# A two-block fp32 transformer kernel: the mixer's column groups, its levels' slots and VectorE's sums of weights in another order

## The chip, the cores and the metric

One core of a Trainium2 chip runs the whole program. The metric is the device time of one execution in microseconds (us); lower is better. The kernel before took 2854.26 us (median of 3 runs).

## What is computed

The reference runs 256 tokens of width 2048, all in fp32, through two transformer blocks. The change lies in the second block's mixer, which works on `hx`, the normalized and modulated tokens, and projects them with `w_in`:

```python
ux, vx, qx, kx, vvx, gx, dfx, dbx = split_proj(hx @ w_in)          # ten column groups of 512
# gated linear attention: 4 heads, keys of 128, values of 256, chunks of 128 tokens, both directions
b = jnp.cumsum(gc, axis=2)
scores = einsum('bhid,bhjd,bhijd->bhij', qc, kc, exp(b_i - b_j))
o = scores @ vc + (qc * exp(b)) @ s
s = exp(b_last) * s + (kc * exp(b_last - b))^T @ vc
# gla_out: rms norm of o, times silu(g);  spatial_gating: gelu(u) * (w_s @ layer_norm(gelu(v)) + b_s)
```

The four lines of the attention are the reference's in meaning, written shorter.

## The kernel before, in words

**Matmuls.** Every large product is cut into column groups of 512, and a group into chunks of 512 rows of the weight. A chunk multiplies 2 x 2 blocks with seven products in place of eight (`chunk`, line 533): 14 fp32 matmuls of 128x256 on TensorE. Four of the seven products use a raw block of the weight (`ring`), three use sums of blocks (`sums`), which VectorE makes two chunks ahead in `step(m)`, lines 962 to 967: two additions, a drain, an addition, a drain, an addition, each over 128x512. `step(m)` waits until the weights of chunk m+2 have landed and until TensorE is through with chunk m-1, so it can begin when chunk m begins. When a group's four chunks are done, VectorE puts its products together in `gather` (lines 979 to 989, four instructions).

**The mixer.** Its 40 slots (g, c) are chunk c of group g. `MIX_GROUPS` gives the order of the groups, and the table `MIX_BESIDE` names for each slot the smaller work that stands beside the chunk. All engines walk the same table. TensorE runs the chunk and then the slot's items. VectorE runs `level_open` of the slot's level if it has one, then `step`, then the items in their order. ScalarE and GpSimd run their part of each item. No scheduler is involved: the order is written out, and an engine that waits holds up all that stands behind it.

**Levels.** The decayed scores of a chunk of tokens are built in eight levels, ("level", n, l) with n = 0, 1 the half of the tokens. For l below 7 a level passes through four engines:

1. VectorE, `level_open` (line 1382, two subtractions): differences of the summed decays into `e_buf`;
2. ScalarE (1880 and 1882): absolute value, then exponential (with a table load ahead of it if a silu or gelu came between);
3. VectorE (`level_close`, 1361 and 1394): takes the previous level's scores out of PSUM, then makes `ql`, queries times decay, in two instructions. GpSimd (2132) makes `kl`, keys times decay, in two instructions, from the same exponential;
4. TensorE (869): four matmuls of 128x128 of `kl` and `ql`, once both are ready.

`level_open` of the next level needs `e_buf` free, so it waits for GpSimd. Level 7 has no decay.

**Other items the texts name.** `upd` (TensorE 857, VectorE 1447, eight instructions): the new states, from the values and the decayed keys. `qt` (TensorE 831, ScalarE 1906): the queries turned. `qe` (ScalarE 1885, VectorE 1460): queries times the summed decays. `o` (TensorE 881 and 883, ScalarE 1924): the output of the attention and its squares. `o_sum`, `o_norm` (VectorE 1469, GpSimd 2121 and 2123, VectorE 1476): its norm and the gate. `y` (TensorE 891) and `y_take` (VectorE 1483): the result turned. `v_mean`, `v_sum`, `v_norm` (VectorE 1490 to 1494, 1500, 1506, with ScalarE and GpSimd between): layer norm of v. `sgu`, `sgu_take` (TensorE 903, VectorE 1406): spatial mixing.

## Time and profile before

| | |
|---|---|
| runs | 2854.8, 2851.78, 2854.26 us; median 2854.26 |
| profiled execution | 2853.87 us, its span 2852.1 us |
| TensorE matmul (PE) busy | 2799.4 us, 98% of the span |
| TensorE weight load (PEld) | 2449.2 us, 86% |
| VectorE (DVE) | 2151.4 us, 75% |
| ScalarE (ACT), GpSimd (POOL) | 396.4 us, 353.2 us |
| mean granted TensorE clock | 0.993 |

Each line of the profile's groups names source line, engine, operation and tiles. `idle before` or a bracket such as [1.84 <-DVE mem L1394] is the time the engine stood still just before, and what ended it. An fp32 matmul counts as two rows of the trace. `mem` is the large buffer that most tiles are cut from, `act_t` and `small` are others, `PS` is PSUM.

### The profile page before, as it was taken

What the parts mean: (1) busy time and instruction counts of PE and PEld (TensorE: products, weight loads), DVE (VectorE), ACT (ScalarE), POOL (GpSimd) and SP (SyncE); (2) the same over time, 40 slices, a digit from 0 to 9 for tenths busy, and PEclk for the clock granted to TensorE, in tenths of its full rate; (3) what the DMA queues carried; (4) which work ended last, traced back from release to release, by engine and by line L of the source; (5) the groups of instructions that cost most, each with busy time, mean ns of one, the idle gap of its engine ahead of it and who ended that gap; (6) DMA issues with size and microseconds to landing.
All of it is one profiled execution on the core that took longest, in us unless ns stands there. A gap on an engine that the chain in (4) does not pass through costs nothing.

```text
span 2852.1 us, 34930 instructions
## 1 busy us (share of the span) xinstructions
PE 2799.4 (98%) x13260; PEld 2449.2 (86%) x13260; DVE 2151.4 (75%) x3355; ACT 396.4 (14%) x703; POOL 353.2 (12%) x438
## 2 busy tenths in 40 slices
PE   8999999999999999999999999999799999999998
PEld 7888888888888888888887888788688888888887
DVE  5888777988999999989886558787676676555554
ACT  2221112001111111100012113310200000000000
POOL 1012231011121121211110001110001110000000
PEclk9999999999999999999999999999899999999999
DMA  8677666677776667677874455447467766566553
GB/s 264 214 254 229 207 203 203 211 247 223 210 213 213 208 207 213 207 250 250 277 242 130 143 156 140 125 155 223 141 214 214 219 214 200 170 160 195 177 173 122
DMA packets 274984, 571.62 MB, mean 200 GB/s; under 512 B 24522, under 2 KB 25432, under 8 KB 274304
## 3 DMA queue, kind: packets, MB, share of 16 engines
q1 hardware_dynamic: 244112, 460.44, 52.4%
q0 software_dynamic: 30416, 108.87, 12.2%
q8 instruction: 105, 1.72, 0.2%
q14 instruction: 63, 0.52, 0.1%
q10 hardware_dynamic: 288, 0.07, 0.0%
HBM read 565.37 MB, written 3.93 MB: 200 GB/s over the span
## 4 chain that ended last, share of the span: by engine, by line
PE 74%; issue 18%; DVE 3%; DVEq 1%; DMA 1%; POOL 1%; ACT 1%; POOLq 0%; ACTq 0%
PE PS L533 69%; PE PS L595 1%; DVEq L964 1%; PE PS L561 1%; DMA ring<-in_w_in 1%; PE PS L731 0%; PE PS L647 0%; PE PS L622 0%; DVE sums L965 0%; DVE sums L967 0%; DVE mem L1053 0%; DMA ring<-in_w_down 0%; DVE sums L962 0%; DVE ring L963 0%; PE PS L869 0%
## 5 line engine op out<-in xcount | busy, mean ns | idle before, releaser
L533 PE MATMUL PS<-sums,mem 128*128 128x256 f32 x4080 | 1216.4, 380 | 0.0
L533 PE MATMUL PS<-ring,mem 128*128 128x256 f32 x3800 | 1075.8, 380 | 1.4 <-DVE sums L967 1.4
L533 PEld LDWEIGHTS PS<-sums,mem 128*128 128x128 f32 x4080 | 777.0, 190 | 106.1
L533 PE MATMUL PS<-ring,act_t 128*128 128x256 f32 x3112 | 845.6, 380 | 3.9 <-DVE sums L967 3.3
L533 PEld LDWEIGHTS PS<-ring,mem 128*128 128x128 f32 x3800 | 719.5, 191 | 99.7 <-DVE sums L967 2.5
L533 PEld LDWEIGHTS PS<-ring,act_t 128*128 128x128 f32 x3112 | 585.5, 191 | 82.2 <-issue 4.6
L962 DVE TENSOR_TENSOR sums<-ring 128x512 f32<-128x512 f32 x432 | 314.2, 727 | 382.7 <-PE PS L533 353.9
L1053 DVE SCALAR_TENSOR_TENSOR mem<-mem,small 128x512 f32<-128x512 f32 x480 | 353.8, 758 | 34.0 <-DMA mem<-in_w_mod 2.7
L965 DVE TENSOR_TENSOR sums<-sums,ring 128x512 f32<-128x512 f32 x432 | 312.3, 723 | 33.4 <-issue 1.3
L967 DVE TENSOR_TENSOR sums<-sums,ring 128x512 f32<-128x512 f32 x432 | 307.6, 712 | 33.2 <-issue 1.4
L533 PE MATMUL PS<-sums,act_t 128*128 128x256 f32 x1104 | 329.2, 380 | 0.0
L2024 POOL DMA_DIRECT2D mem<-in_w_mod x192 | 139.3, 726 | 1497.9 <-DVE mem L1053 1411.4
L963 DVE TENSOR_TENSOR ring<-ring 128x512 f32<-128x512 f32 x432 | 295.9, 685 | 0.0
L533 PEld LDWEIGHTS PS<-sums,act_t 128*128 128x128 f32 x1104 | 210.4, 191 | 28.8
L1605 ACT COPY first_q<-PS 128x256 f32<-128x256 f32 x98 | 36.4, 372 | 993.3 <-PE PS L533 993.3
L979 DVE TENSOR_TENSOR mem<-PS,first_q 128x512 f32<-128x512 f32 x96 | 65.7, 685 | 44.6 <-PE PS L533 44.5
L1252 DVE SCALAR_TENSOR_TENSOR mem<-PS,small,mem 128x255 f32<-128x255 f32 x176 | 76.6, 477 | 3.3
L1776 ACT ACTIVATE mem<-PS,small 128x256 f32<-128x256 f32 x88 | 44.8, 560 | 208.7 <-PE PS L595 208.7
L985 DVE TENSOR_TENSOR mem<-PS,mem 128x512 f32<-128x512 f32 x96 | 66.4, 692 | 9.3 <-issue 0.8
L989 DVE TENSOR_TENSOR mem<-PS,mem 128x512 f32<-128x512 f32 x96 | 66.4, 691 | 9.2 <-issue 0.4
L1768 ACT ACTIVATE mem<-mem,small 128x512 f32<-128x512 f32 x44 | 29.4, 714 | 157.4 <-DVE mem L989 157.4
L1626 ACT ACTIVATE act_t<-PS,small 128x256 f32<-128x256 f32 x64 | 28.8, 517 | 160.5 <-PE PS L561 160.3
(237 smaller groups left out, 1224.7 us busy)
## 6 DMA issues: line engine op xcount, KB each, us to landing
ring<-in_w_in SPq DMA_DIRECT2D x240, 512.0 KB, 3.7
mem<-in_w_mod POOLq DMA_DIRECT2D x192, 512.0 KB, 5.0
ring<-in_w_up SPq DMA_DIRECT2D x176, 512.0 KB, 3.8
ring<-in_w_ffn_in SPq DMA_DIRECT2D x176, 512.0 KB, 3.6
ring<-in_w_down SPq DMA_DIRECT2D x88, 512.0 KB, 4.5
ring<-in_w_ffn_out SPq DMA_DIRECT2D x88, 512.0 KB, 3.8
ring<-in_w_out SPq DMA_DIRECT2D x64, 512.0 KB, 4.3
ring<-in_w_branch_a SPq DMA_DIRECT2D x16, 512.0 KB, 3.7
```

The source lines that it names most:

```text
L533: mm = pe.matmul(product(g, j), of(j, 2 * (c if part is None else part) + q), weights(j, n, q), start=lead and j in OPENS, stop=tail, skip ...
L962: ve.tensor_tensor(to[:, 0], b11, b12, ADD)
L963: ve.tensor_tensor(b12, b22, b12, ADD)
L965: ve.tensor_tensor(to[:, 1], to[:, 0], b22, ADD)
L967: ve.tensor_tensor(to[:, 2], to[:, 1], b21, ADD).then_inc(s["sums_ready"], 1)
L979: ve.tensor_tensor(both(c11, c12), two(Q2), bc(first_q[:, g % 2].unsqueeze(1), [P, 2, 256]), ADD)\
L985: ve.tensor_tensor(both(c12, c22), bc(product(g, Q5).unsqueeze(1), [P, 2, 256]), both(c12, c21), SUB)\
L989: ve.tensor_tensor(both(c12, c21), two(Q3), both(c12, c21), ADD).then_inc(s["acc_free"], 1)
L1053: op = ve.scalar_tensor_tensor(acc[:, which, :], wm[:, h % 2, k, :], col, acc[:, which, :], MUL, ADD)
L1252: op = ve.scalar_tensor_tensor(o, src, conv[:, k, 2 * side:2 * side + 1], o, MUL, ADD)
L1776: op = act.activation(dst[:, 2 * part + f, :], PS[:, 7, f * T:(f + 1) * T], ACT.Identity, scale=conv[:, k, 1:2], bias=conv[:, k, 3:4])
L2024: pool.dma_start(wm[:, h % 2], w_mod[:, kt:kt + 2, col:col + CN]).then_inc(wm_loaded[h % 2], 16)
```

## The change

Three edits, all in the mixer.

1. **Groups.** The order k, q, vv0, vv1, g0, ... becomes k, vv0, vv1, q, g0, ...: the values' two groups come before the queries'. With them `upd` moves from slot (4, 0) to (3, 1) and `qt` from (2, 0) to (4, 0). The waits are changed to match.
2. **Slots of the second half's levels.** Level (1, 0) with its `qe` moves from (6, 3) to (6, 2), ahead of that slot's `o_sum` and `o_norm`; level (1, 1) moves from (7, 0) to (6, 3). `y_take` moves from (7, 0) to (7, 1). Levels (1, 2) and later keep their slots.
3. **`step` in two parts.** In a slot with a level VectorE now runs `level_open`, the first two additions (`step_first`), `level_close`, and then the last two additions (`step_last`), where the whole `step` stood ahead of `level_close`. In the other slots both parts follow each other as before. `level_close` also waits for `q_kept`.

```diff
-        MIX_GROUPS = [("k", 2560), ("q", 2048), ("vv0", 3072), ("vv1", 3584), ("g0", 4096), ("g1", 4608),
+        MIX_GROUPS = [("k", 2560), ("vv0", 3072), ("vv1", 3584), ("q", 2048), ("g0", 4096), ("g1", 4608),
...
-                      (1, 3): [("gather", 1), ("cum",)], (2, 0): [("qt",)], (2, 1): [("rem", 0), ("rem", 1)],
-                      (2, 2): [("wst",)], (2, 3): [("gather", 2)], (3, 0): [("wsum",)], (3, 3): [("gather", 3)],
-                      (4, 0): [("upd", 0), ("upd", 1)], (4, 1): [("level", 0, 0), ("qe", 0)],
+                      (1, 3): [("gather", 1), ("cum",)], (2, 1): [("rem", 0), ("rem", 1)],
+                      (2, 2): [("wst",)], (2, 3): [("gather", 2)], (3, 0): [("wsum",)], (3, 1): [("upd", 0), ("upd", 1)],
+                      (3, 3): [("gather", 3)], (4, 0): [("qt",)], (4, 1): [("level", 0, 0), ("qe", 0)],
...
-                      (6, 1): [("take", 8), ("o", 0)], (6, 2): [("o_sum", 0), ("o_norm", 0)],
-                      (6, 3): [("level", 1, 0), ("qe", 1), ("gather", 6), ("y", 0)],
-                      (7, 0): [("open_v", 0), ("level", 1, 1), ("y_take", 0), ("v_mean", 0)],
-                      (7, 1): [("v_sum", 0), ("v_norm", 0)],
+                      (6, 1): [("take", 8), ("o", 0)], (6, 2): [("level", 1, 0), ("qe", 1), ("o_sum", 0), ("o_norm", 0)],
+                      (6, 3): [("level", 1, 1), ("gather", 6), ("y", 0)], (7, 0): [("open_v", 0), ("v_mean", 0)],
+                      (7, 1): [("y_take", 0), ("v_sum", 0), ("v_norm", 0)],
...
-                        pe.wait_ge(s["cum_kept"], 1)
+                        pe.wait_ge(s["state_ready"], 4)
...
-                            pe.wait_ge(s["state_ready"], 4)
+                            pe.wait_ge(s["q_kept"], 1)
...
             def step(m):
+                step_first(m)
+                step_last(m)
+
+            def step_first(m):
...
                 ve.tensor_tensor(to[:, 0], b11, b12, ADD)
                 ve.tensor_tensor(b12, b22, b12, ADD)
+
+            def step_last(m):
...
                 ve.drain()
                 ve.tensor_tensor(to[:, 1], to[:, 0], b22, ADD)
...
+                ve.wait_ge(s["q_kept"], 1)
...
                 if level:
                     level_open(*level)
-                step(N0["mix"] + 4 * g + c)
+                step_first(N0["mix"] + 4 * g + c)
+                if level:
+                    level_close(*level)
+                    lv += 1
+                step_last(N0["mix"] + 4 * g + c)
...
-                    elif item[0] == "level":
-                        level_close(*level)
-                        lv += 1
```

In the `...` are the moved waits of `rem`, `wst` and `qe` (for `cum_kept` and `q_kept`), the indices `VV_GROUP` and `Q_GROUP`, and the list of the gathers' targets.

**What moves on VectorE around the first level.** VectorE, slots (4, 0) to (4, 2); before:

```order
L1447 SCALAR_TENSOR_TENSOR mem<-mem,small,PS 128x256 x8
L1454 MEMSET mem 128x512
L1382 TENSOR_TENSOR mem<-mem 128x512 x2
L962 TENSOR_TENSOR sums<-ring 128x512
L963 TENSOR_TENSOR ring<-ring 128x2x256
L965 TENSOR_TENSOR sums<-sums,ring 128x512
L967 TENSOR_TENSOR sums<-sums,ring 128x512
L1394 TENSOR_TENSOR mem<-mem 128x4x64 x2
L1460 TENSOR_TENSOR mem<-mem 128x512 x2
L1382 TENSOR_TENSOR mem<-mem 128x512 x2
```

and in the changed program, where lines 1393, 966 to 978, 1406 and 1477 are what 1382, 962 to 967, 1394 and 1460 were:

```order
L976 TENSOR_TENSOR sums<-sums,ring 128x512
L978 TENSOR_TENSOR sums<-sums,ring 128x512
L1393 TENSOR_TENSOR mem<-mem 128x512 x2
L966 TENSOR_TENSOR sums<-ring 128x512
L967 TENSOR_TENSOR ring<-ring 128x2x256
L1406 TENSOR_TENSOR mem<-mem 128x4x64 x2
L976 TENSOR_TENSOR sums<-sums,ring 128x512
L978 TENSOR_TENSOR sums<-sums,ring 128x512
L1477 TENSOR_TENSOR mem<-mem 128x512 x2
L1393 TENSOR_TENSOR mem<-mem 128x512 x2
```

The state update (1447) no longer stands ahead of the first opening, and the queries' part of the level (1394, now 1406) stands in the middle of the step's four additions.

**What moves on VectorE around levels (1, 0) and (1, 1).** VectorE, slots (6, 2) and (6, 3), up to the gather of group 6; before:

```order
L1469 TENSOR_REDUCE small<-mem 128x4
L1476 SCALAR_TENSOR_TENSOR mem<-PS,small,mem 128x256 x4
L1382 TENSOR_TENSOR mem<-mem 128x512 x2
L962 TENSOR_TENSOR sums<-ring 128x512
L963 TENSOR_TENSOR ring<-ring 128x2x256
L965 TENSOR_TENSOR sums<-sums,ring 128x512
L967 TENSOR_TENSOR sums<-sums,ring 128x512
L1394 TENSOR_TENSOR mem<-mem 128x4x64 x2
L1460 TENSOR_TENSOR mem<-mem 128x512 x2
L979 TENSOR_TENSOR act_t<-PS,first_q 128x512
```

and in the changed program, with 1483 and 1490 for 1469 and 1476, 1372 for 1361, 990 for 979:

```order
L1406 TENSOR_TENSOR mem<-mem 128x4x64 x2
L976 TENSOR_TENSOR sums<-sums,ring 128x512
L978 TENSOR_TENSOR sums<-sums,ring 128x512
L1477 TENSOR_TENSOR mem<-mem 128x512 x2
L1483 TENSOR_REDUCE small<-mem 128x4
L1490 SCALAR_TENSOR_TENSOR mem<-PS,small,mem 128x256 x4
L1393 TENSOR_TENSOR mem<-mem 128x512 x2
L966 TENSOR_TENSOR sums<-ring 128x512
L967 TENSOR_TENSOR ring<-ring 128x2x256
L1372 COPY_PREDICATED mem<-mem,PS 128x512
L1406 TENSOR_TENSOR mem<-mem 128x8x32 x2
```

The output's norm (1469, 1476) now stands between two levels, behind level (1, 0) and ahead of the opening of level (1, 1).

## Rows read from the trace of the kernel before

**Rows 1.** TensorE's waits ahead of the levels' matmuls: total, times, longest.

```profile
PE PS L869 <- DVE mem L1394: 7.3, 5, 3.4
PE PS L869 <- POOL mem L2132: 2.6, 1, 2.6
```

**Rows 2.** Timeline of TensorE, the levels' matmuls and a chunk's first: start, length, operation, idle before.

```profile
1733.28 1.57 PE L869 MATMUL PS<-mem 128*128 128x128 f32 x8 [1.84 <-DVE mem L1394]
...
1741.99 1.05 PE L869 MATMUL PS<-mem 128*128 128x128 f32 x8
1742.88 1.03 PE L533 MATMUL PS<-ring,mem 128*128 128x256 f32 x4
...
1748.92 1.05 PE L869 MATMUL PS<-mem 128*128 128x128 f32 x8
...
1756.39 1.16 PE L869 MATMUL PS<-mem 128*128 128x128 f32 x8 [0.36 <-DVE mem L1394]
...
1819.97 1.13 PE L869 MATMUL PS<-mem 128*128 128x128 f32 x8 [2.63 <-POOL mem L2132]
...
1836.63 2.07 PE L869 MATMUL PS<-mem 128*128 128x128 f32 x8 [3.44 <-DVE mem L1394]
```

**Rows 3.** Stretches behind three of these waits; 0.61, 1.00, 0.57 are the granted clock.

```profile
1733.00:1737.00 4.00, 3.72 (x14) 3.28 (x15) 3.91 (x7) 1.09 (x2) 0.00 (x0) 0.61 0.41 138
...
1820.00:1824.00 4.00, 4.00 (x23) 3.64 (x24) 3.76 (x6) 0.68 (x1) 0.00 (x0) 1.00 0.09 35
...
1836.00:1840.00 4.00, 3.37 (x17) 3.37 (x18) 3.77 (x7) 1.94 (x2) 0.00 (x0) 0.57 0.07 25
```

**Rows 4.** Timeline of VectorE around the first level.

```profile
1723.70 3.38 DVE L1447 SCALAR_TENSOR_TENSOR mem<-mem,small,PS 128x256 f32<-128x256 f32 x8 [3.84 <-PE PS L857]
...
1731.41 1.81 DVE L1394 TENSOR_TENSOR mem<-mem 128x256 f32<-128x256 f32 x2
...
1746.28 0.76 DVE L1394 TENSOR_TENSOR mem<-mem 128x256 f32<-128x256 f32 x2 [0.16 <-issue]
```

**Rows 5.** Timeline of VectorE, one level from opening to opening, then the next.

```profile
1763.23 1.29 DVE L1382 TENSOR_TENSOR mem<-mem 128x512 f32<-128x512 f32 x2 [0.62 <-POOL mem L2132]
...
1765.80 0.69 DVE L965 TENSOR_TENSOR sums<-sums,ring 128x512 f32<-128x512 f32 x1
...
1767.17 0.76 DVE L1361 COPY_PREDICATED mem<-mem,PS 128x512 f32<-128x512 int32 x1
1768.09 1.29 DVE L1394 TENSOR_TENSOR mem<-mem 128x256 f32<-128x256 f32 x2 [0.16 <-issue]
```

**Rows 6.** Timelines of ScalarE and GpSimd: queries' copy, a table load, two keys' parts.

```profile
1669.24 1.02 ACT L1906 ACTIVATE mem<-PS 128x1024 f32<-128x1024 f32 x1 [5.05 <-PE PS L831]
...
1804.87 1.28 ACT L1882 ACT_TABLE_LOAD   x1
...
1731.13 1.81 POOL L2132 TENSOR_TENSOR mem<-mem 128x256 f32<-128x256 f32 x2 [52.41 <-ACT mem L1882]
...
1766.88 1.89 POOL L2132 TENSOR_TENSOR mem<-mem 128x256 f32<-128x256 f32 x2 [3.69 <-ACT mem L1882]
```

**Rows 7.** Timeline of VectorE in the second half, slots (6, 2) to (7, 2).

```profile
1797.61 1.22 DVE L1469 TENSOR_REDUCE small<-mem 128x4 f32<-128x1024 f32 x1 [3.34 <-ACT mem L1924]
...
1802.43 1.29 DVE L1382 TENSOR_TENSOR mem<-mem 128x512 f32<-128x512 f32 x2
...
1810.27 0.68 DVE L979 TENSOR_TENSOR act_t<-PS,first_q 128x512 f32<-128x512 f32 x1
...
1813.11 1.29 DVE L1382 TENSOR_TENSOR mem<-mem 128x512 f32<-128x512 f32 x2
...
1819.21 1.21 DVE L1483 TENSOR_TENSOR mem<-PS,small 128x1024 f32<-128x1024 f32 x1
...
1823.20 0.69 DVE L962 TENSOR_TENSOR sums<-ring 128x512 f32<-128x512 f32 x1
...
1830.65 1.29 DVE L1382 TENSOR_TENSOR mem<-mem 128x512 f32<-128x512 f32 x2
```

More of the change, by code:

```diff
@@ L370, in build @@
                                ("sgu", 1, 1)]}
-        K_GROUP, Q_GROUP, VV_GROUP, G_GROUP, V_GROUP, U_GROUP = 0, 1, 2, 4, (6, 8), (7, 9)
+        K_GROUP, VV_GROUP, Q_GROUP, G_GROUP, V_GROUP, U_GROUP = 0, 1, 3, 4, (6, 8), (7, 9)
         def beside(table, groups):
@@ L835, in _ @@
                         r = item[1]
+                        pe.wait_ge(s["cum_kept"], 1)
                         mm = pe.matmul(PS[:, 6 + r, :], tri[:, 2 + r, :], la[:, r, r, :], start=True, stop=True)
@@ L838, in _ @@
                     elif item[0] == "wst":
-                        pe.wait_ge(s["q_kept"], 1)
+                        pe.wait_ge(s["cum_kept"], 1)
                         pe.wait_ge(s["mixer_loaded"], 16)
@@ L960, in step @@
                 w, to = ring[:, n % SLOTS], sums[:, n % TSLOTS]
-                b11, b12, b21, b22 = w[:, :, 0, 0:256], w[:, :, 0, 256:512], w[:, :, 1, 0:256], w[:, :, 1, 256:512]
+                b11, b12, b22 = w[:, :, 0, 0:256], w[:, :, 0, 256:512], w[:, :, 1, 256:512]
                 ve.tensor_tensor(to[:, 0], b11, b12, ADD)
                 ve.tensor_tensor(b12, b22, b12, ADD)
+            def step_last(m):
+                n = m + 2
+                if n >= CHUNKS:
+                    return
+                w, to = ring[:, n % SLOTS], sums[:, n % TSLOTS]
+                b21, b22 = w[:, :, 1, 0:256], w[:, :, 1, 256:512]
                 ve.drain()
@@ L1409, in sgu_take @@
                 op.then_inc(s["sgu_taken"], 1)
-            mix_to = [k_tok, q_tok, vv[:, :, 0:CN], vv[:, :, CN:2 * CN], cat_y[:, :, 0:CN], cat_y[:, :, CN:2 * CN],
+            mix_to = [k_tok, vv[:, :, 0:CN], vv[:, :, CN:2 * CN], q_tok, cat_y[:, :, 0:CN], cat_y[:, :, CN:2 * CN],
                       v2, cat_u[:, :, 0:CN], v2, cat_u[:, :, CN:2 * CN]]
@@ L1457, in _ @@
                         ve.wait_ge(s["qe_exp"], n + 1)
+                        ve.wait_ge(s["q_kept"], 1)
                         qe4 = qe.rearrange("p r (h i) -> p r h i", i=P)
```

## The prediction

> **What bounds the kernel now.** The page's busy times come first: TensorE's matmuls fill 98% of the span, so only what shortens its standing time, or its half-speed time, can help. The number of matmuls does not change. TensorE's waits come next [rows 1]: 7.3 + 2.6 = 9.9 us of standing lie ahead of the levels' matmuls, all between 1730 and 1862 us. The timeline shows the longest of them, 1.84, 2.63 and 3.44 us [rows 2]. Where nothing is late, a level follows the one before by 1748.92 - 1741.99 = 6.93 us: 0.89 until the chunk's first matmul at 1742.88, and 6.04 for the chunk [rows 2].
>
> The waits cost more than their length. From 1733.28 to 1741.99, one level and one chunk, TensorE took 8.71 in place of 6.93 us, though it stood nowhere: the granted clock there is 0.61, and it is 0.57 behind the wait of 3.44 us, so much of both stretches ran at the lower of the clock's levels, 1.2 GHz and not 2.4 [rows 2, 3]. Behind the wait of 2.63 us it is 1.00. I put the loss at 1.8 us behind the first (8.71 - 6.93) and, by the share of 4 us at half speed (twice 0.43 of 4 us, halved, 1.7), some 1.5 behind the third, which began to run at 1836.63, inside the stretch. Together the mixer loses 9.9 + 3.3 = 13.2 us, 0.46% of the run, and no version of this change can win more.
>
> **What sets a level's time.** From the start of an opening to the start of the keys' part it takes 1766.88 - 1763.23 = 3.65 us (two subtractions, absolute value, exponential), and the keys' part takes up to 1.9 us [rows 5, 6]. With 0.1 to TensorE a level is ready (**R**) 5.5 us after its opening starts, or 6.8 with a table load of 1.28 us [rows 6].
>
> **Part 3, the step in two.** Before, VectorE ran 2.57 us of opening and first additions, 1.37 of last additions and 0.92 of taking the scores before the queries' part began [rows 5], which so ended at 4.9 + 1.3 = 6.2 us after the opening's start. Now the queries' part begins with the exponential, at 3.65, and ends at 5.0. The keys' part, which ends at 5.5, becomes the last. That is 0.7 us of gain wherever the queries' part was last. The last additions follow, 1.37 and a drain of 0.16, so the next opening can start 3.65 + 1.3 + 1.5 = 6.5 us after this one. TensorE needs 6.93 per level: the chain gains 0.45 us per level on TensorE, and loses whatever else VectorE has to do between two levels. The weights' sums come 1.3 us later, but they are for a chunk more than 6 us off, so they cost nothing; if that cover went, TensorE would wait for them instead.
>
> **Part 1, values first, and the first half.** Count from T, where TensorE ends the turned queries. Their copy ends at T + 1.2 (1.02 us, and 0.2 for the handover [rows 6]). The opening has run long before, since the state update's 3.38 us [rows 4] no longer stand ahead of it. Absolute value and exponential take 2.3, so the keys' part ends at T + 5.4, and TensorE comes at T + 6.05: **the wait of 1.84 us and the 1.8 us of half speed behind it go**. The moved `upd` and the moved `qt` do their work beside chunks with no level; TensorE does the same matmuls in another slot, and VectorE's stand-by of 3.84 us ahead of the update [rows 4] shows how idle it is there: nothing for the move.
>
> But VectorE sets the pace from there. It ends the queries' part at T + 4.8, the last additions at 6.3, `qe` (two like an opening's, 1.3) at 7.6. Level 1 opens at T + 7.6, ready 13.1, due 6.05 + 6.93 = 13.0: wait 0.1. Level 2 opens at 14.1, no wait. Between it and level 3 stands a gather, 1813.11 - 1810.27 = 2.8 us [rows 7]: level 3 opens at 23.4, is ready at 28.9, and is due at 13.1 + 13.9 = 27.0: **wait 1.9** (0.36 before, since TensorE itself came late). Level 4 opens at 29.9, has a table load behind the silu, is ready at 36.7, due 35.9: **wait 0.8**. The first half waits 2.8 us after 2.2: the standing has moved, and what is left of the gain is the clock.
>
> **Part 2, the second half.** Count from U, the end of the attention's output on TensorE. Level (1, 0) opens 0.2 later, with a table load behind the squares, ready U + 7.0, due U + 6.05: **wait 1.0**. VectorE ends the queries' part at U + 6.4, its additions at 7.9, `qe` at 9.2. Now the norm stands ahead of the next opening, and it includes a trip to GpSimd: 1802.43 - 1797.61 = 4.8 us [rows 7]. Level (1, 1) opens at U + 14.0, ready 19.5. TensorE is due at 7.0 + 0.9 + 6.05 = 14.0: **wait 5.5**. Count from V, the start of that level's matmuls. VectorE is through its additions at V + 0.9, gather 3.7, step 6.4 (twice 1.37), then `v_mean` and `y_take`, 1823.20 - 1819.21 = 4.0 together, and the next step with `v_sum`, its trip to GpSimd and `v_norm` 7.45 (1830.65 - 1823.20). Level (1, 2) opens at V + 17.9 [rows 7]. It now has the gelu behind the previous level, so a table load: ready V + 24.7. TensorE has two small items of 0.9 and three chunks, due V + 19.9: **wait 4.8**, in place of 3.44. Count from W, where that level starts. Level (1, 3) opens at W + 0.9 and is in time. Behind it come `sgu_take` and a gather. `sgu_take` is four instructions of 128x128 from PSUM; eight of twice the width took 3.38 us [rows 4], so it lies between 0.8 and 1.7, and I take 1.0, nearer the half width. Level (1, 4) opens at W + 0.9 + 6.5 + 1.0 + 2.8 = 11.2, ready 16.7, due two chunks and four small items on, 15.6: **wait 1.1**. Level (1, 5) opens at 11.2 + 6.5 + 1.0 = 18.7, with a table load behind the gelu of u, ready 25.5, due 16.7 + 6.9 = 23.6: **wait 1.9**.
>
> **The sum.** After: 0.1 + 1.9 + 0.8 + 1.0 + 5.5 + 4.8 + 1.1 + 1.9 = 17.1 us of waits for 9.9: **+7.2**. Clock: 3.3 us go. Both long waits are longer than the 3.44 that was followed by half speed; the lost 1.7 us of each partly disappear, since the next wait ends when VectorE does, and I keep 1.3 for the two. The waits of 1.9 lie between 1.84, with half speed behind it, and 2.63, without: half of 1.4 for the pair, 0.7. So -3.3 + 2.0 = -1.3, and 7.2 - 1.3 = **+5.9**, on the profiled execution's own 2853.87: **2859.8 us**. Its median of runs is 2854.26, 0.4 above. The bound between no change and slower, about what a measurement of this kernel can tell, is 0.2% or 5.7 us, so 2860.0: the forecast lies on it.
>
> **Contention, not seen alone.** Queries' and keys' parts now start together at every level. At level (0, 0) they did so before: VectorE's pair took 1.81 us from 1731.41 where a pair alone took 0.76, GpSimd's took 1.81 from 1731.13, no more than elsewhere [rows 4, 6]. I take the keys' part at 1.9 and the queries' at 1.3. Bounds: if GpSimd gives way, its part ends up to 0.8 later (the pair alone), if VectorE does, it pays 0.5 more, 1.81 for 1.3, at each of 14 levels; where VectorE's chain sets the pace that is up to 0.5 for each of the 4 levels ahead of level (0, 4) and the 6 of the second half, 5 us at the worst. If neither gives way, 0.5 us less per level, and some 3 us come off.
>
> The Trainium skill (SBUF — State Buffer, "Who interferes with whom") states that a VectorE instruction with two inputs in SBUF and a GpSimd instruction that reads SBUF exclude each other, and the later one fully blocks. By it the keys' part could be last by 0.76 us more, once in each half, 2861.3 us; the 1.81 us above agree for VectorE, and no row shows GpSimd blocked.
>
> **Rivals.**
>
> *A, the chain is the same length in any order.* If VectorE's work from `o` to the last level sets that stretch before and after, then moving its norm behind a level gives the wait at (6, 3) and takes it back later: the second half costs what it did, the first half +0.6 - 1.8, and the end is 2852.7 us, not slower. For it: VectorE is the last to be ready at most waits [rows 1]. Against: VectorE stood 3.34 us ahead of 1797.61 [rows 7] and the ScalarE legs (3.65) are not beside its work if it has none. It decides from the point where the waits at (6, 3) and (7, 2) together fall under the 6.1 us of before.
>
> *B, the clock stays up* behind both long waits, as behind the 2.63 us: 2.0 less, 2857.8 us, no change. Against: rows 3.
>
> *C, GpSimd or VectorE gives way* at each level: +2 to +5, 2863 us. For it: 1.81 against 0.76.
>
> *D, the moved pieces do nothing*: the chunk matmuls hide all but the first level's wait, 2853.87 - 3.6 = 2850.3 us. It needs level (1, 1) ready 5 us sooner than counted; nothing in the rows gives that.
>
> **How the numbers follow.** My forecast 0.65, of which 0.33 above the bound and 0.32 below; A 0.10, nearly all within 0.2%, 0.02 faster; B 0.10, within; C 0.11, slower; D 0.04, half faster. Faster by over 0.2%: 0.05 with a remainder; within: 0.50; slower: 0.45. The range leaves out D, most of A and the worst of C: 2853.0 to 2865.5.
>
> **What would show it.** TensorE's first level without a wait and clock 1.0 behind it; waits of about 1.9 and 0.8 at levels (0, 3) and (0, 4); 5.5 and 4.8 us at (1, 1) and (1, 2), the opening of (1, 1) behind the norm; clock near 0.6 behind both; 17 us of waits ahead of the levels in all. I am wrong if the wait at (1, 1) is under 3 us, or if waits for `sums` appear.

## The result and the profile after

The changed kernel takes 2864.88 us (median of 5 runs, 2859.66 to 2868.45); the kernel before took 2851.78 us beside it (5 runs, 2847.77 to 2854.8). The ratio is 1.004, 95% interval 1.003 to 1.0051: **slower by 0.4%**, some 11.4 us (the medians alone differ by 13.1). The forecast was 2859.8 us, +5.9, on the line between no change (0.50) and slower (0.45). The slower side came, and the time lies inside the range, 0.6 us from its end; the forecast difference is half of the measured one.

The profiled execution of the changed kernel is its fastest run, 2859.66 us, and the one of before (2853.87) is among its slower ones. Two whole profiled executions therefore differ by 5.8 us and hide half of the effect. So I compare one stretch: from the chunk of slot (4, 1) to the second turn of the result (`y`, line 891), which in both programs holds all levels. Stretch by stretch view, first of before, then of after; the columns are length, busy time of PE, PEld, DVE, ACT and POOL with counts, granted clock, share of the DMA engines, GB/s:

```profile
1725.22:1901.00 175.78, 165.85 (x825) 146.03 (x824) 142.57 (x225) 54.25 (x53) 32.82 (x38) 0.98 0.46 134
```

```profile
1720.78:1907.09 186.31, 168.92 (x826) 146.72 (x825) 143.12 (x217) 54.92 (x54) 34.92 (x38) 0.96 0.45 127
```

The stretch grows by 186.31 - 175.78 = **10.5 us**, near the 11.4 of the ratio. It begins 4.4 us earlier in the profiled run of after; such differences come from run to run. In e9 below, whose program is the changed one up to level (1, 1), it begins at 1729.23, 8.5 us later than in after, and the 15 to 30 runs of before beside each set of experiments spread over 8 to 16 us.

TensorE's waits in this stretch, after (before: 9.9 us [rows 1]); total, times, longest:

```profile
PE PS L869 <- POOL mem L2146: 9.3, 2, 5.6
PE PS L869 <- DVE mem L1406: 5.7, 5, 1.7
PE PS L532 <- DVE mem L990: 0.9, 2, 0.6
PE PS L750 <- DVE mem L1527: 0.9, 1, 0.9
PE PS L532 <- DVE mem L996: 0.7, 2, 0.5
```

That is 17.5 us. One by one, in TensorE's timeline of after (start, length, operation, idle before; as [rows 2]):

```profile
1726.83 1.05 PE L869 MATMUL PS<-mem 128*128 128x128 f32 x8
...
1734.59 1.16 PE L869 MATMUL PS<-mem 128*128 128x128 f32 x8 [0.67 <-DVE mem L1406]
...
1751.40 1.13 PE L869 MATMUL PS<-mem 128*128 128x128 f32 x8 [1.41 <-DVE mem L1406]
...
1814.55 2.05 PE L869 MATMUL PS<-mem 128*128 128x128 f32 x8 [5.57 <-POOL mem L2146]
...
1840.00 2.04 PE L869 MATMUL PS<-mem 128*128 128x128 f32 x8 [3.68 <-POOL mem L2146]
...
1867.02 1.13 PE L869 MATMUL PS<-mem 128*128 128x128 f32 x8 [1.67 <-DVE mem L1406]
```

| wait ahead of | forecast | measured |
|---|---|---|
| level (0, 0) | 0 | 0 (before 1.84) |
| level (0, 1) | 0.1 | 0.67 |
| levels (0, 3), (0, 4) | 1.9, 0.8 | 1.41, 1.03 |
| level (1, 0) | 1.0 | 0.96 |
| level (1, 1) | 5.5 | 5.57 |
| level (1, 2) | 4.8 | 3.68 (before 3.44) |
| levels (1, 4), (1, 5) | 1.1, 1.9 | 0, 1.67 |
| chunks behind a late gather, and `open` | none | 1.6 and 0.9 |
| sum | 17.1 | 17.5 (before 9.9) |

So the sum of the waits was forecast to within half a microsecond, and yet the time was not. The nearness of the sum is in part luck: the places with a forecast hold 15.0 of their 17.1 us, and 2.5 us stand where none was forecast. The clock behind the two long waits (as [rows 3]):

```profile
1814.00:1818.00 4.00, 3.45 (x16) 3.48 (x17) 3.65 (x6) 0.02 (x1) 0.45 (x1) 0.51 0.00 0
1840.00:1844.00 4.00, 4.00 (x18) 3.91 (x19) 3.83 (x7) 1.30 (x2) 0.00 (x0) 0.50 0.00 0
```

Half speed, 1.2 GHz, throughout. Matmuls are busy 168.92 - 165.85 = 3.1 us longer for the same work. The books of TensorE are then: waits +7.6, and 2.9 more, which are the half-speed pieces (the forecast had -1.3 for the clock) and the breaks at 12 stops where there were 6.

The two halves of the stretch, cut at the chunk behind the attention's output (1796.36 in before, 1794.64 in after), differ in how well they were forecast:

| | before | after | difference | forecast |
|---|---|---|---|---|
| first half | 71.14 | 73.86 | +2.7 | -0.85 (waits +0.6, clock -1.8 + 0.35) |
| second half | 104.64 | 112.45 | +7.8 | +6.75 (waits +6.6, clock -1.5 + 1.3 + 0.35) |

Most of the miss, 3.6 of 4.6 us, lies in the first half, which was to gain and lost. But books on TensorE only say where it stood. Who made it stand is read on VectorE.

One level on VectorE, after, from opening to opening (as [rows 5]):

```profile
1760.90 1.29 DVE L1393 TENSOR_TENSOR mem<-mem 128x512 f32<-128x512 f32 x2
...
1764.54 1.41 DVE L1406 TENSOR_TENSOR mem<-mem 128x256 f32<-128x256 f32 x2 [0.49 <-ACT mem L1896]
1766.04 1.15 DVE L976 TENSOR_TENSOR sums<-sums,ring 128x512 f32<-128x512 f32 x1
1767.27 0.69 DVE L978 TENSOR_TENSOR sums<-sums,ring 128x512 f32<-128x512 f32 x1
1768.05 1.29 DVE L1393 TENSOR_TENSOR mem<-mem 128x512 f32<-128x512 f32 x2
```

The queries' part starts 3.64 us after the opening, as forecast (3.65), and VectorE stands 0.49 us for it, since it has nothing else to do. Then the addition at line 976 takes 1.15 us where the same addition took 0.69 [rows 5], because it now begins beside GpSimd's keys' part, which runs from 1764.55 to 1766.65 (shown further down). The level takes 1768.05 - 1760.90 = **7.15 us**. Before, it was 6.25, to the next opening:

```profile
1769.48 1.29 DVE L1382 TENSOR_TENSOR mem<-mem 128x512 f32<-128x512 f32 x2
```

(1769.48 - 1763.23, whose start is in [rows 5]). 7.15 is also more than the 6.93 that TensorE needs for a level and its chunk: the chain that should have gained 0.45 us per level on TensorE loses 0.2. This is one of the longer levels. From (0, 3) to (0, 4), where the addition takes 1.04 us, it is 6.91 (1745.79 to 1752.70) for 6.02 before (1750.41 to 1756.43): 0.9 us more again, and no gain on TensorE. Where a table load stands in ScalarE's leg it is worse: 8.20 us behind the openings of (0, 4) and (1, 2) and 8.42 behind that of (1, 5), for 6.80, 6.02 and 7.03 before, with 1.78 us of standing; VectorE, after, at level (1, 2):

```profile
1838.02 1.29 DVE L1406 TENSOR_TENSOR mem<-mem 128x256 f32<-128x256 f32 x2 [1.78 <-ACT mem L1896]
```

VectorE's waits over the stretch, first before, then after:

```profile
DVE mem L1394 <- ACT mem L1882: 1.5, 4, 0.9
```

```profile
DVE mem L1406 <- ACT mem L1896: 14.4, 13, 2.7
```

From 1.5 to 14.4 us: the two additions that used to fill ScalarE's 3.65 us now stand behind it. At one place TensorE hands the pace over anew: the opening of level (1, 0) waits for the attention's output (883), so what VectorE lost before it has already been paid by TensorE, and the second chain starts there.

```profile
1794.91 1.29 DVE L1393 TENSOR_TENSOR mem<-mem 128x512 f32<-128x512 f32 x2 [8.65 <-PE PS L883]
```

### The profile page after: what moved, and what is told of

The parts are those of the page before. It is cut to its first block, busy times and chain, and to the rows that moved or that the text cites. A ratio compares the mean times of both kernels' runs of the same rounds, so it can differ in the third digit from the quotient of the medians.

```text
span 2857.9 us, 34936 instructions
## 1 busy us (share of the span) xinstructions
PE 2799.7 (98%) x13260; PEld 2447.7 (86%) x13260; DVE 2155.6 (75%) x3355; ACT 396.0 (14%) x703; POOL 356.3 (12%) x438
## 4 chain that ended last, share of the span: by engine, by line
PE 75%; issue 18%; DVE 2%; DMA 1%; ACT 1%; DVEq 1%; POOL 1%; POOLq 0%; ACTq 0%
PE PS L532 70%; DMA ring<-in_w_in 1%; PE PS L594 1%; PE PS L560 1%; DVE sums L976 1%; DVEq L975 0%; PE PS L730 0%; PE PS L646 0%; PE PS L621 0%; ACT mem L1896 0%; ACT mem L1894 0%; DVEq L1374 0%; DVE sums L978 0%; PE PS L739 0%; PE PS L636 0%
```

## The experiments

Each ran beside the kernel before, 5 to 12 executions of its own and 15 to 30 of before; "us" is the median, and "ratio" that to before with its 95% interval. "Part 1" is the order of the groups, "Part 2" the slots, "Part 3" the step in two.

| run | what it is | us | ratio |
|---|---|---|---|
| e1_groups_only | before + Part 1 | 2854.11 | 1.0005 (0.9996 to 1.0014) |
| e2_slots_only | before + Part 2 | 2856.55 | 1.0011 (1.0002 to 1.002) |
| e3_split_only | before + Part 3 | 2864.28 | 1.0036 (1.0023 to 1.005) |
| e7_after_whole_step | change - Part 3 | 2855.67 | 1.0011 (1.0002 to 1.002) |
| e8_after_three_one | change, step split 3 + 1 | 2857.67 | 1.0013 (1.0004 to 1.0021) |
| e9_fill | change + idle matmuls in the long waits | 2864.46 | 1.0039 (1.0025 to 1.0053) |
| e4_y_take_late | Part 1, `y_take` late | 2851.62 | 0.9992 (0.9983 to 1.0001) |
| e5_groups_store | Part 1, gate's store early | 2849.83 | 0.9981 (0.9972 to 0.9991) |
| e6_y_late_store | Part 1, both | 2846.01 | 0.9973 (0.9962 to 0.9983) |
| e10_before_store | before, gate's store early | 2852.92 | 0.9998 (0.999 to 1.0007) |
| e11_after_store | change, gate's store early | 2865.16 | 1.0044 (1.0031 to 1.0056) |
| e12_best_three_one | e6, step split 3 + 1 | 2850.05 | 0.9995 (0.9986 to 1.0005) |

### The three parts alone: e1, e2, e3

Each is the kernel before with one edit of the diff above and nothing else of it:

```diff
e1: MIX_GROUPS, and in MIX_BESIDE
-  (2, 0): [("qt",)] ... (4, 0): [("upd", 0), ("upd", 1)]
+  (3, 1): [("upd", 0), ("upd", 1)] ... (4, 0): [("qt",)]
e2: in MIX_BESIDE
-  (6, 3): [("level", 1, 0), ("qe", 1), ...], (7, 0): [..., ("level", 1, 1), ("y_take", 0), ...]
+  (6, 2): [("level", 1, 0), ("qe", 1), ...], (6, 3): [("level", 1, 1), ...], (7, 1): [("y_take", 0), ...]
e3: in VectorE's loop
-  step(m); ...; level_close(*level)
+  step_first(m); level_close(*level); step_last(m)
```

> Part 1 alone: values ahead of queries, the step whole, the second half's levels in their old slots. Theory N (the norm ahead of level (1, 1) is the cost, part 2): the first half gains the first level's wait (1.84 us) and the half speed behind it, the rest is as before; 3 to 4 us faster than before (ratio 0.9987). Theory S (the step in two parts is the cost, part 3, because VectorE now stands for ScalarE's exponential in the middle of every step): the same here, since the step is whole; no wait over 0.6 us ahead of any level of the first half, where the change had 1.4 and 1.0. They differ in what is then missing: under N part 1 with part 3 would be as good as this, under S it would not. A rival of both: the values' place costs by itself, and this is slower than before.

> Part 2 alone: levels (1, 0) and (1, 1) and y_take in the new slots, queries first, the step whole. Theory N: carries nearly the whole loss, +7 to +11 us. Theory S: carries about half, +4 to +5 us: waits of 3.6 us at level (1, 1) (VectorE runs the norm, 4.8 us, between two levels) and 3.7 at (1, 2), against 2.6 and 3.4 before; the first half as before, 1.84 us at the first level.

> Part 3 alone: queries first, old slots, the step in two parts around level_close. Theory N, and the prediction's reading (the queries' part 1.3 us earlier, additions later but hidden): 0 to 2 us faster. Theory S: +6 to +8 us: VectorE stands 0.5 us per level for the exponential, 1.8 us where a table load is in it, and gathers and take-overs come later; waits of about 1.6 and 0.9 us at levels (0, 3) and (0, 4), 2.9 and 4.8 us at (1, 1) and (1, 2).

**e3** is nearly the whole loss: +0.36%, 10.3 us where theory S had 6 to 8, with the old order of the groups and the old slots. TensorE's waits, and VectorE's, with Part 3 alone:

```profile
PE PS L869 <- DVE mem L1405: 11.0, 8, 2.7
PE PS L869 <- POOL mem L2144: 3.3, 1, 3.3
```

```profile
DVE mem L1405 <- ACT mem L1894: 12.7, 14, 2.4
```

and one level on VectorE, from opening to opening:

```profile
1766.68 1.29 DVE L1393 TENSOR_TENSOR mem<-mem 128x512 f32<-128x512 f32 x2
...
1770.30 1.41 DVE L1405 TENSOR_TENSOR mem<-mem 128x256 f32<-128x256 f32 x2 [0.46 <-ACT mem L1894]
1771.80 1.15 DVE L976 TENSOR_TENSOR sums<-sums,ring 128x512 f32<-128x512 f32 x1
...
1773.81 1.29 DVE L1393 TENSOR_TENSOR mem<-mem 128x512 f32<-128x512 f32 x2
```

From opening to opening 1773.81 - 1766.68 = 7.13 us, the 7.15 of the changed kernel again: the long cycle belongs to Part 3, whatever the order around it.

**e2** costs +0.11%, 3.1 us (0.6 to 5.7). The part that the prediction charged with 5.5 and 4.8 us brings waits of 4.6 and 3.7 us, but a sum of only 12.6 in place of 9.9. Its profiled stretch is 180.47 us, 4.7 more than that of before; how much of this is clock is taken up at e9.

**e1** makes no difference that can be told, where 3 to 4 us of gain were expected. The first level's wait goes as forecast, but 2.65 us appear one level later, and behind them stands a load of weights; VectorE's timeline in e1:

```profile
1735.92 1.27 DVE L967 TENSOR_TENSOR sums<-ring 128x512 f32<-128x512 f32 x1 [2.97 <-DMA ring<-in_w_in]
```

### The change without the split, and with another split: e7, e8

```diff
e7:
-                step_first(N0["mix"] + 4 * g + c)
+                step(N0["mix"] + 4 * g + c)
                 if level:
                     level_close(*level)
                     lv += 1
-                step_last(N0["mix"] + 4 * g + c)
e8: step_first also makes the third addition
+                ve.drain()
+                ve.tensor_tensor(to[:, 1], to[:, 0], b22, ADD)
```

> The change without part 3: the step whole, all else as changed. Theory S (the step in two): 3 to 5 us above before (ratio 1.001 to 1.002), waits of 3.6 to 4.6 us at (1, 1) and 3.7 at (1, 2), none for gathers. Theory N (the norm between the levels): 8 to 11 us above before, like the change itself.

> The change with the step divided three to one: three additions ahead of the level's close, one behind. VectorE then reaches the close about 4.2 us after the opening's start, when ScalarE's exponential (3.65) is done, so it no longer stands for it, save where a table load is in it. Theory S: 3 to 4 us faster than the change (ratio to before 1.003 in place of 1.004), the 0.5 us stands gone. If contention between the queries' and the keys' part made the loss, it stays at 1.004.

e7 takes the loss from +0.4% to +0.11%. Its stretch, and its VectorE's wait for the exponential:

```profile
1724.57:1902.20 177.63, 164.19 (x827) 144.84 (x826) 138.28 (x217) 55.16 (x54) 32.44 (x38) 0.99 0.48 133
```

```profile
DVE mem L1406 <- ACT mem L1895: 2.8, 5, 1.2
```

Set beside the rows of the change above, these price the split. From e7 to the change the stretch grows by 186.31 - 177.63 = 8.7 us. VectorE's busy time grows by 143.12 - 138.28 = 4.8 us for the same 217 rows of the trace, and its idle time by 43.2 - 39.4 = 3.8 us: it stands 11.6 us more for the exponential (14.4 - 2.8) and some 8 us less for other things: for TensorE to free `sums` (4.7 to 1.8), for GpSimd to free `e_buf` (2.0 to 0) and for weights (3.0 to 1.4). That last one is not free in e7: TensorE stands 2.66 us behind it at level (0, 1), as in e1. Nearly all of the busy time is one line, the third addition; the groups of VectorE's instructions in this stretch (count, busy us, mean ns, idle before), in e7 and in the changed kernel:

```profile
L976 DVE TENSOR_TENSOR sums<-sums,ring 128x512 f32<-128x512 f32 x22 | 15.2, 693 | 1.6
```

```profile
L976 DVE TENSOR_TENSOR sums<-sums,ring 128x512 f32<-128x512 f32 x22 | 20.2, 919 | 1.9
```

e8, with three additions ahead of the close and one behind, lies near e7 (1.0013 and 1.0011; the intervals cover each other); 3 to 4 us of gain on the change were expected, and it is more, 0.27%. The profiled stretches order the three more finely:

| | stretch | VectorE busy | VectorE's wait for the exponential |
|---|---|---|---|
| e7, step whole | 177.63 | 138.28 | 2.8 |
| e8, three and one | 180.07 | 141.91 | 6.6 |
| change, two and two | 186.31 | 143.12 | 14.4 |

From the change to e8 the stretch gives back 6.2 of the 8.7 us, while VectorE's busy time falls by only 1.2 and its wait for the exponential by 7.8. So of what the split costs, the larger part goes with the standing and not with the longer instructions; the 2.4 us that remain between e8 and e7 come with 3.6 us more of busy time.

### Is it the half speed? e9

```diff
+            FILL = {(1, 1): 22, (1, 2): 16}
...
                     elif item[0] == "level":
+                        for _ in range(FILL.get(item[1:], 0)):
+                            pe.matmul(PS[:, 5, 0:P], ident[:], ident[:], start=True, stop=True)
```

TensorE multiplies the identity by itself into a bank that nobody reads while it would stand still ahead of levels (1, 1) and (1, 2).

> The change, with 22 matmuls of 128x128 of the identity by itself (4.8 us) ahead of the wait at level (1, 1) and 16 (3.5 us) ahead of that at (1, 2), into a bank nobody reads then: TensorE works while it waits, and comes no later. If the half speed behind both waits is what the change loses over its waits, the clock stays at 1.00 there and it is 2 to 5 us faster than the change (ratio to before 1.0025 to 1.003). If the stretch is set by VectorE alone, the half speed was hidden and the time stays within 1 us of the change.

The clock stays up, and nothing is gained: ratio 1.0039 against 1.004. The two places behind the waits, then the whole stretch of e9:

```profile
1823.00:1827.00 4.00, 3.99 (x26) 3.52 (x27) 3.65 (x7) 0.07 (x1) 0.00 (x0) 1.00 0.02 4
1848.00:1852.00 4.00, 4.00 (x27) 3.74 (x28) 3.83 (x7) 1.39 (x2) 0.00 (x0) 1.00 0.01 4
```

```profile
1729.23:1915.58 186.35, 175.30 (x903) 153.05 (x902) 143.25 (x217) 54.94 (x54) 34.88 (x38) 0.99 0.45 127
```

186.35 against 186.31 us. VectorE is busy 143.25 against 143.12. TensorE ran faster and then stood longer; level (1, 5) now waits

```profile
1874.92 2.04 PE L872 MATMUL PS<-mem 128*128 128x128 f32 x8 [2.28 <-DVE mem L1409]
```

where it waited 1.67 in the change. From the start of level (1, 2) to that of level (1, 5) both programs take 27.02 us (1840.00 to 1867.02 and 1847.90 to 1874.92). The 0.6 us that e9 gains from (1, 1) to (1, 2) it loses behind the wait of 2.28, where its clock falls to 0.58 and the level takes 2.04 us for 1.13. So in the second half of the changed kernel VectorE's chain has the length: speed given to TensorE is handed back as a wait.

This holds for the divided step alone. e2 and e7 have the whole step and the same program in the second half, with waits of 4.57 at (1, 1) and 3.67 and 3.69 at (1, 2). Behind the second one the granted clock is 0.50 in e2 and 1.00 in e7, and from (1, 2) to (1, 5) they take 26.67 and 23.83 us, with 0.96 and 0.99 us of wait at the end. There 2.8 us of half speed are paid in full, and they are more than half of the 4.7 us by which e2's stretch exceeds that of before.

### What holds Part 1 back: e4, e5, e6, e10, e11

In the order of the weight loads the store of the gate (`store_gate(0)`, line 468: 8 KB, written element by element to rows that are not contiguous) stands behind the loads of group 4. In before no engine waits for a load in this stretch; with Part 1 the first level opens earlier, VectorE comes to the next step earlier, and finds its weights not there. SyncE's queue in e1, and the landing times of that store (min, median, max):

```profile
1715.39 3.39 SPq L437 DMA_DIRECT2D ring<-in_w_in  x2
1718.82 0.81 SPq L468 DMA_DIRECT2D gate_rows<-small  x1
1721.43 17.25 SPq L437 DMA_DIRECT2D ring<-in_w_in  x6
```

```profile
DMA to landing us min/median/max: 13.0/13.2/13.3
```

```diff
e5 = e1 with, e10 = before with, e11 = change with:
-                if g == 4:
+                if g == 1:
                     store_gate(0)
e4 = e1 with:
-                      (7, 0): [("open_v", 0), ("level", 1, 1), ("y_take", 0), ("v_mean", 0)],
+                      (7, 0): [("open_v", 0), ("level", 1, 1), ("v_mean", 0)],
...
-                      (8, 3): [("level", 1, 7), ("u_take", 0, 1), ("gather", 8)],
+                      (8, 3): [("level", 1, 7), ("u_take", 0, 1), ("gather", 8), ("y_take", 0)],
e6 = e1 with both
```

> Not a part of the change: part 1 alone, and y_take of the first half moved from (7, 0) to (8, 3), where VectorE has room. If VectorE's own work between the levels sets the second half's waits, the waits at (1, 1) and (1, 2) fall to about 2.3 and 1.9 us, neither long enough for half speed as a rule, and it is 5 to 8 us faster than before (ratio 0.998). If the norm's trip to GpSimd or ScalarE's table loads set them, it is as part 1 alone.

> Part 1 alone, and the store of the first gate's 8 KB (2048 single numbers, 12 us to land) moved from behind group 4's weights to behind group 1's. In part 1 alone TensorE stood 2.65 us at level (0, 1), because VectorE stood 2.97 us for the weights of chunk (5, 0), the first load behind that store. If the store delays that load, the wait at level (0, 1) goes, and it is 2 to 5 us faster than before (ratio 0.9985 to 0.999). If the load is late for another reason (the landing of the weights in general), the wait stays and the time is as part 1 alone.

> The moved store with part 1 and the late y_take: the candidate for the best. By the same reasoning 6 to 8 us faster than before (ratio 0.9975), waits of 0.6 us or less in the first half, of 2.6 and 2.1 at (1, 1) and (1, 2). If the store is not the cause: as with the late y_take alone, ratio 0.999.

> The kernel before with the gate's store moved as in the runs above. There no engine stood for weights behind it, since TensorE came 2 us later at the first level. If the store only matters where the chain has caught up with it: no change (ratio 0.9995 to 1.0005). If a moved store is worth 3 us anywhere, 0.999.

> The change with the moved store. Its own wait for weights was 1.40 us on VectorE, and TensorE's wait of 0.67 at level (0, 1). The chain behind it is VectorE's, so 1 to 2 us faster than the change (ratio to before 1.003 to 1.0037); as much as the 3.7 us that it gave part 1 alone only if late weights weigh more in most executions than in the profiled one.

With the store early, Part 1 does what it was predicted to: e5 has no wait at levels (0, 0) and (0, 1), and is faster than before by 0.19%. The store alone does nothing for before (0.9998), so the two belong together: Part 1 wins the first level's wait, and the store's queue had taken that back. The half speed behind that wait is not a sure gain: e2 and e10 run the program of before up to there, stand 1.85 us, and have a granted clock of 1.00 behind it. The first half takes 71.14 us in before, 69.97 in e10, 70.47 in e1 and 67.35 in e5. TensorE's waits in e5:

```profile
PE PS L870 <- DVE mem L1407: 5.3, 4, 3.4
PE PS L870 <- POOL mem L2146: 2.7, 1, 2.7
```

In e4 and e6 `y_take` (1.21 us on VectorE) no longer stands between levels (1, 1) and (1, 2) but behind the last level. The wait of 3.4 falls to 2.1, with half speed behind it still (granted clock 0.57 and 0.61). e4 was expected to be 5 to 8 us faster than before and cannot be told from it (0.9983 to 1.0001). e6 takes **2846.01 us, 0.27% less than before**, the lowest median of all, though its interval overlaps that of e5; its stretch is 1.1 us shorter than e5's:

```profile
PE PS L870 <- DVE mem L1407: 3.9, 4, 2.1
PE PS L870 <- POOL mem L2146: 2.7, 1, 2.7
```

e11 was a miss: I expected the early store to help the changed kernel by 1 to 2 us, and it gives nothing (1.0044). The wait at level (0, 1) fell from 0.67 to 0.26 us and all the later ones stayed. The first half is 0.40 us shorter for it (73.46 for 73.86), and the second 0.5 longer, with the clock at 0.50 for 0.58 in the 4 us from the start of level (1, 1). So the saving is carried on, but 0.4 us is far below what the medians can tell; the expectation had taken VectorE's own wait of 1.40 us for it.

### The other split on the best order: e12

The edit is that of e8 on e6.

> The fastest version so far (values first, y_take(0) late, the gate's store early: 2846.0 us, 0.9973 of before) with the step of the sums split three additions ahead of the level's close and one behind. Theory (in this stretch VectorE's own chain sets the time, and a split gains only where the queries' part does not wait for ScalarE): the exponential is done 3.65 us after the opening starts, three additions and taking the scores end at about 4.1 to 4.2, so hardly any wait for ScalarE, and the queries' part is 0.7 us earlier, but the chain per level is no shorter: 2845 to 2849 us, waits ahead of levels 6 to 9 us. Rival (the split helps, the two-two one only went too far): the levels become ready earlier and waits fall by 2 us or more: 2842 to 2844. Rival (any split costs, by contention of the queries' part with the keys' part): 2850 or more.

2850.05 us, above the 2845 to 2849 that the theory gave, just where the rival of contention began (2850), and 0.2% over e6. Its stretch, to set beside that of e6, which comes first:

```profile
1722.14:1892.78 170.64, 164.04 (x826) 144.89 (x825) 138.30 (x217) 55.16 (x54) 32.74 (x38) 0.99 0.47 136
```

```profile
1723.88:1897.81 173.93, 165.18 (x827) 144.64 (x826) 141.67 (x217) 55.14 (x54) 32.13 (x38) 0.99 0.46 133
```

The stretch is 3.3 us longer and VectorE's busy time 3.4. The queries' part and the addition behind it carry it, first e6 and then e12:

```profile
L1407 DVE TENSOR_TENSOR mem<-mem 128x256 f32<-128x256 f32 x28 | 17.5, 666 | 4.5 <-ACT mem L1896 2.8 <-issue 1.7
...
L979 DVE TENSOR_TENSOR sums<-sums,ring 128x512 f32<-128x512 f32 x22 | 15.2, 692 | 1.6
```

```profile
L1407 DVE TENSOR_TENSOR mem<-mem 128x256 f32<-128x256 f32 x28 | 20.0, 756 | 8.3 <-ACT mem L1897 6.6 <-issue 1.7
L979 DVE TENSOR_TENSOR sums<-sums,ring 128x512 f32<-128x512 f32 x22 | 17.5, 797 | 1.9
```

These two lines grow by 4.8 us, and the others give 1.4 back. The split moves VectorE's two-input work under GpSimd's keys' part, and the instructions that lie there are longer. e8 has the same loss against e7, 2.4 us of stretch for 3.6 of busy time; its median is 2.0 us over e7's.

## Why the prediction was right, and where it was wrong

**Right: the longest waits and, in part by luck, the sum.** 17.1 forecast, 17.5 measured, with 5.5 against 5.57 us at level (1, 1), whose opening stands behind the norm as said. That the sum fits owes 2.5 us to waits nobody forecast, which make up for 2.1 that did not come. That the time lies in the range is luck too: it is 0.6 us from the end, and the cost came from the part that was to help. The first level's wait went. The terms of ScalarE's leg (3.65, measured 3.64) and of the norm and the gather were sound. No waits for `sums` appeared on TensorE.

**Wrong: the step "the chain gains 0.45 us per level on TensorE".** It failed in three ways.

1. *Its comparison.* The text priced the new cycle at 6.5 us and set it beside TensorE's 6.93. The row to set it beside was VectorE's own old cycle, 6.25 us, opening to opening. By the prediction's own numbers Part 3 lengthened VectorE's chain by 0.2 us at this level, and by 0.5 where the old cycle was 6.02; that it did not help was there to be read.
2. *Its size.* The cycle is 6.91 to 7.15. Of the 0.65 more at the longer one, 0.46 is the addition beside the keys' part (1.15 for 0.69), 0.12 the queries' pair (1.41 for 1.29), the rest gaps between instructions. "The last additions follow, 1.37" took their duration from rows in which they began while GpSimd was idle.
3. *Its attribution.* Part 2 was to carry the loss and Part 3 to pay back. Part 3 alone costs 0.36%, Part 2 alone 0.11%, and the change without Part 3 0.11%. The waits of 5.5 and 4.8 stand at places that Part 2 made; with the whole step e7 has 4.6 and 3.7 there. Rival A (the second half costs what it did) is out by its own test, which wanted the two under 6.1 us together: they are 9.25 in the change and 8.24 in e2.

**Wrong: the clock's -1.3.** Both long waits had half speed behind them (rival B is out: 0.51 and 0.50). Of the 1.8 us that were to go behind the first level, e2 and e10 show that they are not always there: after the same stop a level and its chunk take 7.21 us at clock 1.00 for 8.71, so half speed was 1.5 of them, in one profiled execution of three. And e9 removes the half speed of the second half and wins nothing, so in the changed kernel the terms for it should have been 0 either way (B's price of 2.0 us with them), though not with the whole step, as e2 and e7 show. The prediction added a clock term to waits that end when VectorE does; the same sentence that let "the lost 1.7 us of each partly disappear, since the next wait ends when VectorE does" should have been applied to all of it.

**Contention.** The forecast took the queries' part at 1.3 and bounded the case that VectorE gives way at 0.5 us per level, "5 us at the worst". VectorE's busy time rose by 4.8 us between e7 and the change. Rival C, with 0.11, was in its kind what happened, on VectorE's side, and its place was above all not the queries' part but the addition behind it: a third instruction with two inputs in SBUF, which Part 3 put there. The prediction read GpSimd as not held up, since its pair took 1.81 us "no more than elsewhere" [rows 4, 6]. But elsewhere it stood beside VectorE too. Alone, while VectorE waits for weights, one instruction of GpSimd's pair takes 0.73 us (e7, at 1734.68). The single instructions of level (0, 3) in the change:

| start | us | ends | |
|---|---|---|---|
| 1749.43 | 0.42 | 1749.85 | VectorE, queries' part, first |
| 1749.44 | 0.99 | 1750.43 | GpSimd, keys' part, first |
| 1749.77 | 0.94 | 1750.71 | VectorE, queries' part, second |
| 1750.40 | 0.90 | 1751.30 | GpSimd, keys' part, second |
| 1750.80 | 1.04 | 1751.85 | VectorE, the addition |

VectorE's second ends 0.28 us after GpSimd's first, and the addition 0.55 us after GpSimd's second. These two distances are the same in all 14 and 13 such rows of the change, whatever the lengths. GpSimd's two end 0.58 us after VectorE's first and second. The rule weighed in the prediction (the Trainium skill, SBUF — State Buffer, "Who interferes with whom"), that the later of the two is fully blocked until the other is through, agrees with these rows, instruction by instruction and in both directions. Pairs hide this: one pair seems merely slower, 1.29 to 1.41 us for 0.76, and the other likewise,

```profile
1764.55 2.10 POOL L2146 TENSOR_TENSOR mem<-mem 128x256 f32<-128x256 f32 x2 [5.06 <-ACT mem L1896]
```

for 1.41 us alone. What the prediction missed in applying it was the addition: 0.35 us more at nine levels and 0.46 at four are the 5.0 us by which its line grew.

**Not counted at all.** TensorE's waits for the gathers (1.6 us), since the last additions now stand ahead of them; the breaks around each stop, of which there were twice as many; and the late weights behind the gate's store, which took away the gain that Part 1 was credited with. That last one was in the trace of before, in the list of DMA issues, and I did not look at what a moved item's loads queue behind. It does not bear on the changed kernel's time (e11), only on why Part 1 looks worthless.

**How 5.9 became 10.5.** The excess is 4.6 us in the stretch, 3.6 of it in the first half and 1.1 in the second. In the first half e10 and the change both have the clock at 1.00: TensorE's matmuls are busy 67.53 and 69.20 us, so its breaks cost 1.7, and its waits are 2.4 and 4.7. To this comes the half speed of before, of which 1.2 us show between its first half and e10's. In VectorE's terms, its level costs 0.4 to 0.65 us more than forecast, and the blocked addition is 0.35 to 0.46 of that, 5.0 us over 13 levels. That this is the cause of the excess is worked out and not shown, since no run had the split without the contention. It is not the cause of the whole loss: e8 keeps 3.6 of the 4.8 us of longer instructions and loses only 2.4 of the 8.7 us of stretch.

## What to carry to other kernels

An engine that waits for another's result in the middle of its own chain should have its filler work ahead of the wait, not behind it: compare the new cycle with the same engine's old one, not with the engine downstream. When TensorE's waits all end with VectorE, count VectorE's time from opening to opening and treat TensorE's clock and small waits as free in both directions (e9), but only then: with VectorE's chain shorter the same half speed cost 2.8 us (e2 and e7). A few dummy matmuls in the wait test this cheaply. Where an instruction is moved beside another engine's, look at single instructions and not at pairs. When an item is moved earlier, look at what its loads queue behind: here a store of 8 KB stood ahead of them, and moving it turned a change worth nothing into 0.2%.

## What was new about the hardware

- Idle matmuls (22 and 16 of 128x128) ahead of a wait held the granted clock at 1.00 through both places that had 0.51 and 0.50, and saved nothing; behind the next wait, 2.28 us, it fell to 0.58.
- A store of 8 KB to non-contiguous rows takes 13 us to land and holds back weight loads of 512 KB issued behind it on the same queue by about 3 us at the consumer, while the loads' usual landing takes 3.8 us (median of 240). The store and the loads are of one queue; that the store's many small pieces are the reason was not tried apart.
- Beside GpSimd's two-input instructions those of VectorE wait one by one, and the waiting lies inside their duration, not in the idle time ahead: in the change each ends 0.28 us (128x256) or 0.55 us (128x512) after GpSimd's, so that an addition of 0.69 us takes 1.04 to 1.15. GpSimd's own takes 0.73 alone and up to 1.12 beside VectorE.
- The length of a stop alone does not tell whether half speed follows, and the same stop differs between executions. Half speed (granted clock 0.50 to 0.61) stood behind stops of 1.84 (before), 2.13 (e6), 2.28 (e9) and 5.57 us (the change), and clock 1.00 behind 1.85 (e2, e10), 2.63 (before) and 3.11 us (e4). A stop of 2.66 us had 0.57 behind it in e3 and 1.00 in e5, and one of 3.67 to 3.69 us had 0.50 in e2 and the change and 1.00 in e7 and e8.
